# A decoder layer on one core: the row products with w_out take eight merged pairs, their weight sums formed in the gates stage and stored

## What is computed

```python
merged = (jax.nn.sigmoid(g_sb) * (o_sb @ w_branch[:SB_W])
          + jax.nn.sigmoid(g_ds) * (o_ds @ w_branch[SB_W:]))
x = x + merged @ w_out

h = rms_norm(x, ffn_norm_g)
u = causal_depthwise_conv(h @ w_up, conv_w, conv_b)
```

## Time and profile before

| | us |
|---|---|
| median of 3 runs | 1435.23 (1435.18 to 1435.26) |
| profiled execution, its own time | 1435.17 |
| its span, first to last instruction | 1433.3 |

### The profile page before, as it was taken

The page is one execution under the profiler, slowest core; times in us unless marked ns, Lnnn a source line. Parts: engine busy times, 40 slices in busy tenths (PEclk is TensorE's granted clock), DMA queues, the critical chain, the costliest instruction groups (busy, mean ns, idle before and its releaser), DMA issues.

```text
span 1433.3 us, 23700 instructions
## 1 busy us (share of the span) xinstructions
PE 1427.8 (100%) x7626; PEld 1222.9 (85%) x7626; DVE 1138.3 (79%) x1503; ACT 841.5 (59%) x1181; POOL 448.0 (31%) x493
## 2 busy tenths in 40 slices
PE   9999999999999999999999999999999999999999
PEld 7888888888888888888888888888888888888887
DVE  6778998886656566899967778777778778999998
ACT  7545667666767666666664455455554545465553
POOL 2310000333132213650025455655556555200000
PEclk9999999999999999999999999999999999999999
DMA  8565665655554545567555565566665565566664
GB/s 260 187 197 172 209 195 186 193 176 176 161 162 160 167 170 178 189 221 234 192 178 184 183 202 181 186 191 190 190 191 185 180 198 185 192 232 206 204 207 148
DMA packets 121063, 272.25 MB, mean 190 GB/s; under 512 B 10688, under 2 KB 10976, under 8 KB 121008
## 3 DMA queue, kind: packets, MB, share of 16 engines
q1 hardware_dynamic: 119936, 268.99, 58.1%
q0 software_dynamic: 896, 2.42, 0.6%
q10 hardware_dynamic: 176, 0.14, 0.0%
HBM read 269.42 MB, written 2.10 MB: 189 GB/s over the span
## 4 chain that ended last, share of the span: by engine, by line
PE 99%; DMA 0%; DVE 0%; DVEq 0%; issue 0%
PE bank L2098 98%; PE bank L2152 1%; DMA y<-in_x 0%; PE bank L2371 0%; PE bank L2412 0%; DVE y L1770 0%; PE bank L2235 0%; PE bank L2171 0%; PE bank L2213 0%; DVE y L1815 0%; DVEq L201 0%; PE bank L2220 0%; PE bank L2210 0%; PE bank L2202 0%; DVEq L529 0%
## 5 line engine op out<-in xcount | busy, mean ns | idle before, releaser
L1100 DVE TENSOR_TENSOR lo<-raw,hi 128x1024 fp32r<-128x1024 f32 (+1 forms) x342 | 444.3, 1304 | 167.0 <-ACT hi L639 166.3
L639 ACT ACTIVATE hi<-raw 128x1024 fp32r<-128x1024 f32 (+1 forms) x342 | 359.2, 1053 | 271.6 <-PE bank L2098 266.9
L2098 PE MATMUL bank<-h2T,hi 128*128 128x512 f32 x1408 | 483.3, 394 | 0.0
L2098 PE MATMUL bank<-h2T,lo 128*128 128x256 f32 x1408 | 376.8, 278 | 0.0
L2098 PEld LDWEIGHTS bank<-h2T,hi 128*128 128x128 f32 x1408 | 257.9, 188 | 53.5
L2098 PE MATMUL bank<-hT,hi 128*128 128x512 f32 (+1 forms) x784 | 272.9, 395 | 0.0
L2098 PEld LDWEIGHTS bank<-h2T,lo 128*128 128x128 f32 x1408 | 264.4, 188 | 7.8
L2098 PE MATMUL bank<-hT,lo 128*128 128x256 f32 (+1 forms) x784 | 212.6, 281 | 0.0
L2062 POOL TENSOR_TENSOR u<-u,rms_row 128x256 f32<-128x256 f32 x88 | 120.9, 1374 | 184.7 <-DVE u L1621 165.7
L2098 PE MATMUL bank<-hi,ffT 128*128 128x512 f32 x576 | 177.4, 389 | 0.0
L2098 PEld LDWEIGHTS bank<-hT,hi 128*128 128x128 f32 (+1 forms) x784 | 143.9, 187 | 29.4
(11 more groups left out here) (292 smaller groups left out, 2017.6 us busy)
## 6 DMA issues: line engine op xcount, KB each, us to landing
raw<-in_w_up SPq DMA_DIRECT2D x176, 512.0 KB, 3.5
raw<-in_w_in SPq DMA_DIRECT2D x160, 512.0 KB, 3.4
raw<-in_w_down SPq DMA_DIRECT2D x88, 512.0 KB, 4.4
raw<-in_w_branch SPq DMA_DIRECT2D x32, 512.0 KB, 3.6
raw<-in_w_out SPq DMA_DIRECT2D x24, 512.0 KB, 4.6
raw4h<-in_w_in SPq DMA_DIRECT2D x8, 512.0 KB, 3.4
raw5h<-in_w_in SPq DMA_DIRECT2D x8, 512.0 KB, 4.4
raw45m<-in_w_out SPq DMA_DIRECT2D x8, 512.0 KB, 4.9
```

Of the source, the lines that this page charges most:

```text
L639: act.activation(hi[s][:, 0:width], raw[s][:, 0:width], ACT.Copy)\
L1100: dve.tensor_tensor(lo[s][:, 0:width], raw[s][:, 0:width], hi[s][:, 0:width].bitcast(f32), ALU.subtract)\
L2098: return pe.matmul(o, l, r, start=start, stop=stop, skip_group_check=True)
```

## The change

- `OUT_SUMMED` goes from 3 to 4: four merged and four plain pairs in each block. The stage has 48 chunks for 44, and 48 raw loads for 32.
- The sums of w_out's blocks are no longer made in the out stage. In the gates stage SP loads, once a head, the four blocks of one merged pair and half into a buffer `out_pre` (1 MB in three loads, ahead of the first weight load of the group), DVE adds at j = 5 (1024 wide), 6 and 7 (512 wide each), and SP writes the 1 MB to an array in HBM, `out_sums` (ahead of the group's seventh load). Eight such turns, for four pairs and two halves. SP waits for a turn's store before the next turn's loads, and for the last before branch group 1.
- In the out stage a merged pair takes four loads: 256 KB, 512 KB, and two of 512 KB from `out_sums`. Its chunks are then all made alike.
- The order of the pairs changes, with two places in each block where two merged pairs, 0 and 1 or 2 and 3 (in block 1 only 2 and 3), follow each other. `out_sums(m, n)` is called `out_far(m, n)`; its offsets for block 0, those of `out_near` and of `square` change. For block 1 the offsets (7, 8, 9, 10) stay, counted from a pair that starts at chunk 40 of 48 for 34 of 44.
- The last eight raw loads (for the last four) rotate over slots 0 to 3.

```diff
--- before.py
+++ after.py
-    OUT_SUMMED = 3
+    OUT_SUMMED = 4
...
-    OUT_ORDER = [[("plain", 4)] + turns(0, 5, 1, 6, 2, 3) + [("plain", 7)],
-                 turns(0, 4, 1, 5, 2, 6) + [("plain", 3), ("plain", 7)]]
-    ROW_STEPS = block_steps({b: ROW_ORDER for b in S_BLOCKS}, ROWS_AT[2], 0)
+    OUT_ORDER = [[("plain", 4), ("summed", 0), ("summed", 1), ("plain", 5), ("summed", 2), ("summed", 3),
+                  ("plain", 6), ("plain", 7)],
+                 [("summed", 0), ("plain", 4), ("summed", 1), ("plain", 5), ("summed", 2),
+                  ("summed", 3), ("plain", 6), ("plain", 7)]]
...
-    ROW_SLOT += [q if q < SLOTS else q % SLOTS if q >= OUT_RAWS - SLOTS else q % (SLOTS + 2)
-                 for q in range(OUT_RAWS)]
+    ROW_SLOT += [q if q < SLOTS else q % (SLOTS + 2) if q < SLOTS + (SLOTS + 2) * OUT_EXTRA
+                 else q % SLOTS for q in range(OUT_RAWS)]
...
+        out_pre = at("out_pre", [4 * GRP], 48 * KB)
+        out_sums = nc.dram_tensor("out_sums", (2 * OUT_SUMMED * P, 4 * GRP), f32,
+                                  kind="Internal").ap()
...
-                for k in range(2):
+                for k in range(4 if step.stored else 2):
...
+                    width = GRP if step.stored and k == 0 else BLOCK
+                    if k < 2:
+                        kt = 2 * step.pair + k
+                        src = w[kt * P:(kt + 1) * P, ds(col, width)]
+                    else:
+                        row = (2 * step.pair + step.m - NB) * P
+                        src = out_sums[row:row + P, (k - 2) * BLOCK:(k - 1) * BLOCK]
+                    load(slot, raw_s[stage(step)][slot][:, 0:width], src)
...
+            def out_turn(pair, m):
+
+                i = 2 * pair + m
+                row, col = 2 * P * pair, m * BLOCK
+
+                def before(j):
+                    if j == 0:
+                        wait_alone(sp, out_stored, 16 * i + 1)
+                        sp.dma_start(out_pre[:, 0:2 * GRP], w_out[ds(row, P), col:col + BLOCK])\
+                            .then_inc(out_landed, 16)
+                        sp.dma_start(out_pre[:, 2 * GRP:3 * GRP],
+                                     w_out[ds(row + P, P), col + GRP:col + BLOCK])\
+                            .then_inc(out_landed, 16)
+                        sp.dma_start(out_pre[:, 3 * GRP:4 * GRP],
+                                     w_out[ds(row + P, P), col:col + GRP])\
+                            .then_inc(out_landed, 16)
+                    if j == 6:
+                        wait_alone(sp, out_summed, 3 * i + 3)
+                        sp.dma_start(out_sums[ds(P * i, P), :], out_pre[:, :])\
+                            .then_inc(out_stored, 16)
+                return before
+
+            prime(sp, out_stored)
+            load_group(C_GATES, w_in, 0, GATE_AT)
+            with sp.Fori(0, OUT_SUMMED - 1) as q:
+                for m in range(2):
+                    load_group(C_GATES, w_in, CPG * (2 * q + m + 1), GATE_AT + GRP * (2 * q + m + 1),
+                               before=out_turn(q, m))
+            load_group(C_GATES, w_in, CPG * 7, GATE_AT + GRP * 7, before=out_turn(OUT_SUMMED - 1, 0))
+            load_group(C_BRANCH, w_branch, 0, 0, before=out_turn(OUT_SUMMED - 1, 1))
+            wait_alone(sp, out_stored, 16 * 2 * OUT_SUMMED + 1)
+            with sp.Fori(1, 4) as g:
                 load_group(C_BRANCH, w_branch, CPG * g, GRP * g)
...
-                if 18 <= c - OUT_AT[1] < 22:
-                    square(c - OUT_AT[1] - 18)
+                if 21 <= c - OUT_AT[1] < 25:
+                    square(c - OUT_AT[1] - 21)
...
-                    first_at = step.chunk - (1 if stage(step) else 2)
-                    second_at = step.chunk + (1 if stage(step) and step.made == 1
-                                              else 0 if stage(step) else -1)
-                    b1, b2 = [raw_s[stage(step)][ROW_SLOT[step.raw + k]] for k in range(2)]
-                    s13, s24 = ssum13[stage(step)], ssum24[stage(step)]
-                    if c == first_at:
+                    b1, b2 = [raw_s[0][ROW_SLOT[step.raw + k]] for k in range(2)]
+                    s13, s24 = hsum13, hsum24
+                    if c == step.chunk - 2:
...
+                    if j == 5:
+                        dve.wait_ge(out_landed, 48 * h + 48)
+                        dve.tensor_tensor(out_pre[:, 0:2 * GRP], out_pre[:, 0:2 * GRP],
+                                          out_pre[:, GRP:3 * GRP], ALU.add).then_inc(out_summed, 1)
+                    if j == 6:
+                        dve.wait_ge(out_summed, 3 * h + 1)
+                        dve.tensor_tensor(out_pre[:, 2 * GRP:3 * GRP], out_pre[:, 0:GRP],
+                                          out_pre[:, 2 * GRP:3 * GRP], ALU.add)\
+                            .then_inc(out_summed, 1)
+                    if j == 7:
+                        dve.wait_ge(out_summed, 3 * h + 2)
+                        dve.tensor_tensor(out_pre[:, 3 * GRP:4 * GRP], out_pre[:, 2 * GRP:3 * GRP],
+                                          out_pre[:, 3 * GRP:4 * GRP], ALU.add)\
+                            .then_inc(out_summed, 1)
...
-                    weight_sums(c)
...
-                weight_sums(c)
-                for m, joins_at in enumerate(((7, 10, 16, 22), (7, 8, 9, 10))):
+                for m, joins_at in enumerate(((7, 12, 13, 18), (7, 8, 9, 10))):
                     if c - FAR_LAST[NB + m] in joins_at:
-                        out_sums(m, joins_at.index(c - FAR_LAST[NB + m]))
-                if c - OUT_AT[1] in (16, 17):
-                    for o in ((0, 1), (2, 3))[c - OUT_AT[1] - 16]:
+                        out_far(m, joins_at.index(c - FAR_LAST[NB + m]))
+                if c - OUT_AT[1] in (11, 20):
+                    for o in (0, 1) if c - OUT_AT[1] == 11 else (2, 3):
                         out_near(o)
```

More of the change, by code:

```diff
@@ L69, in hybrid_layer @@
     C_ROWS = KT // TAIL_CK
-    Step = namedtuple("Step", "m pair made chunk raw")
+    Step = namedtuple("Step", "m pair made chunk raw stored", defaults=(False,))
     S_BLOCKS = range(2, NB)
@@ L86, in hybrid_layer, with block_steps @@
     BLOCK_END = {**{b: ROWS_AT[b + 1] for b in S_BLOCKS}, NB: OUT_AT[1], NB + 1: OUT_AT[2]}
-    def block_steps(orders, chunk, raw):
+    def block_steps(orders, chunk, raw, stored):
         table = []
@@ L93, in block_steps @@
                 made = pair if kind == "summed" else None
-                table.append(Step(b, pair, made, chunk, raw + 2 * len(table)))
+                table.append(Step(b, pair, made, chunk, raw, stored and made is not None))
                 chunk += 2 if made is None else 4
+                raw += 4 if table[-1].stored else 2
             assert chunk == BLOCK_END[b]
@@ L537, in load, with load_group @@
                 sp.dma_start(dst, src).then_inc(w_landed[slot], 16)
-            def load_group(c0, w, step, col, n=CPG, width=GRP, per=CK):
+            def load_group(c0, w, step, col, n=CPG, width=GRP, per=CK, before=None):
                 for j in range(n):
+                    if before is not None:
+                        before(j)
                     wait_alone(sp, lo_done, c0 + j - AHEAD + step)
@@ L577, in load_step @@
                         wait_alone(sp, sig_done, 8 * 4)
-                    kt = 2 * step.pair + k
-                    load(slot, raw_s[stage(step)][slot][:, :],
-                         w[kt * P:(kt + 1) * P, ds(col, BLOCK)])
+                    width = GRP if step.stored and k == 0 else BLOCK
[6 more added lines that the diff above has]
+                    load(slot, raw_s[stage(step)][slot][:, 0:width], src)
             for step in ROW_STEPS:
@@ L1233, in weight_sums @@
                             dve.wait_ge(lo_done, ROW_S[n - 1].chunk + 3)
-                        dve.wait_ge(left_done, 2 * stage(step) + 2)
+                        dve.wait_ge(left_done, 2)
                         slot = ROW_SLOT[step.raw]
-                        if slot < SLOTS or stage(step):
-                            both = (raw_two + [raw45m])[slot // 2]
+                        if slot < SLOTS:
+                            both = raw_two[slot // 2]
                             dve.tensor_tensor(s13[:, :].rearrange("p (n c) -> p n c", n=2),
```

47 lines of the change are left out of this document (24 added, 23 removed).

## The result

The changed kernel takes **1439.5 us** (median of 9 runs, 1438.6 to 1440.7) against 1435.2 for the kernel before; the ratio is 1.0026, with a 95% interval of 1.0018 to 1.0035. That is slower by about 4 us (4.2 by the medians, 3.7 by the ratio), and the whole interval lies above 1. The profiled execution took 1439.72 us by its own time, the one of before 1435.17.

The account below looks back on a forecast made before the run. PE was taken to bound the kernel, busy 1427.8 of 1433.3 us. From 1435.2 us, the terms -1.4 + 0.4 + 0.7 + 0.6 + 0.8 + 2.0 = +3.1 gave 1438.3 us, range 1436.3 to 1441.0.

Parts of the forecast that it names:

- Removed matmuls: Out stage: two more merged pairs save a product of three matmuls each on PE, -1.4 us.
- The gates stage: Gates stage: the added loads, additions and stores fit in idle time and cost PE 0.
- Start of the out stage: Chunks 7 to 9 fall behind as subtractions slow while POOL mixes, +0.4 us (0 to +1).
- Load 43: End of out stage: load 43 waits for lo 39 and lands 3.5 us later; PE waits, +0.7 us (0.5 to 1.5).
- rival C: Loads bound the merged runs: 5 us a load, pairs 2 and 3 of block 0 also lose; 1440.8 us, chance 0.19.
- Far copies: End of out stage: ACT's last far copy holds up PE's eight transposes, +0.6 us (0 to 1).
- h2T: Start of up stage: PE's first chunk waits for DVE's first h2T tile, +0.8 us (0.3 to 1.3).
- banks: Up stage: PE's first transposes wait for DVE to add the near banks, +2.0 us (1 to 3).
- A: Backlog at the end of the out stage as the terms have it: 1438.3 us, 1437.0 to 1440.0, chance 0.6.
- B: End of out stage hidden, far additions fit, hi 47 3 us earlier than t = 15.4: 1434.7 us, chance 0.12.
- D: Gates stage pays 0.3 to 0.5 us a head for late bank sums or stores: 1441.3 us, chance 0.05.
- E: Nothing moves but the matmuls, no new waits at the out stage's end: 1433.8 us, chance 0.04.

Follow-up runs that it names:

- stored3: Kernel before plus the stored sums only: three merged pairs, old pair order, additions and squares at old places; 1435.9 us, ratio 0.9997.
- gates_only: Kernel before plus the change's gates-stage loads, additions and stores, with the stored sums read by nobody; 1435.5 us, ratio 1.0000.
- slots6: Changed kernel with the last eight out-stage loads kept rotating over six raw slots; 1439.5 us, ratio 1.0018.
- order2: Changed kernel with block 1's pairs reordered so the last merged pair ends two chunks earlier; 1440.4 us, ratio 1.0031.
- both: Changed kernel with six raw slots to the end and the last merged pair two chunks earlier; 1438.0 us, ratio 1.0013.
- far_last: Changed kernel with DVE's end order changed: h2T, two far-addition sets, four banks, lo 50, last two sets; 1442.7 us, ratio 1.0048.
- far_slots_order: `far_slots` with block 1's pairs ordered summed 0, plain 4, summed 1, 2, plain 5, summed 3, plain 6, 7; 1441.2 us, ratio 1.0037.
- far_slots: `far_last` with six raw slots to the end of the out stage; 1440.5 us, ratio 1.0038.
- banks_slots: Changed kernel with six slots, first h2T tiles ahead of the third far-addition set and banks ahead of the fourth; 1439.0 us, ratio 1.0021.
- spread: Changed kernel with six slots and block 1's end work (far additions, h2T tiles, squares) spread over the up stage; 1436.8 us, ratio 1.0013.

## Why the prediction came out

1438.3 us was predicted, between 1436.3 and 1441.0; 1439.5 was measured. Step by step:

- **Removed matmuls, -1.4**: right. `stored3` without waits takes 109.3 with 366 matmuls; 360 take 1.36 less.
- **The gates stage, 0**: right, by `gates_only`. SP's wait for the store was the part without a row. The store of 1 MB lands 4.7 us after its issue, as soon as the loads (4.8). The Trainium skill ("DMA: Bandwidth & Descriptors", section "Anatomy of one DMA - SWDGE (gpsimd) path") warns of a long confirmation where the target is HBM; no run here shows one beyond a load's.
- **Start of the out stage, +0.4**: wrong in sign, by 0.7 to 0.8. PE lost nothing at chunks 7 to 9, and the small waits of before (0.4) went too. I let POOL mix until 637 us as before; it ends at 633.4 now, and from 632.7 on four subtractions take 1.2 us each (the first, still beside POOL, is only 512 wide; such a one takes 0.68 elsewhere, as at 688.75; the other three are 1024 wide):

```profile
626.25 1.77 DVE L1262 TENSOR_TENSOR lo<-raw,hi 128x1024 fp32r<-128x1024 f32 x1 [0.52 <-ACT hi L767]
632.70 4.78 DVE L1262 TENSOR_TENSOR lo<-raw,hi 128x512 fp32r<-128x512 f32 x4
...
631.83 1.54 POOL L2087 TENSOR_TENSOR br<-br,br 128x256 f32<-128x256 f32 x1
```

  The Trainium skill ("SBUF - State Buffer", section "Who interferes with whom") has a VectorE instruction with two inputs in SBUF contend with a GpSimd instruction that reads SBUF. The trace agrees: 1.77 us beside POOL and 1.2 without. With DVE's sums gone POOL's mixing ends sooner too, which the step left out; `gates_only` and `stored3`, whose out stages start at the same 626.4 us, show it by the last instruction of the mixing:

```profile
637.20 1.54 POOL L2083 TENSOR_TENSOR br<-br,br 128x256 f32<-128x256 f32 x1
...
632.96 0.74 POOL L2085 TENSOR_TENSOR br<-br,br 128x256 f32<-128x256 f32 x1
```
- **Load 43, +0.7**: the step that failed in size. It measured 2.3, as 0.95 at chunk 41 and 1.36 at 43. The place and the cause (look-ahead of four slots) were right, as `slots6` shows; the landing time was not. I took 3.5 us, the median of the up stage's loads, for loads that are issued four in a row, though the 24 loads of w_out into slots 0 to 3 have a median of 4.6 us on the page of before. They took 5.0, 5.1 and 5.3 (rival C's number), and load 41 was late as well.
- **Far copies, +0.6; h2T, +0.8; banks, +2.0**: 0.3, 1.3 and 1.6, together 3.1 where 3.4 was said. DVE without a gap and the two waits that DVE ends are as predicted; the last far copy ended at 703.72 and the eight transposes started at 703.77, as predicted too, but so small a wait has no releaser in the views. `order2` and `both` show them as one thing: with the last merged pair two chunks earlier all three are gone.
- **Chunk 20, 0.3**: not in the sum. It is a late load of block 0, and one of the signs that I had named for C was there: loads issued from 636 to 648 us took 5.9 to 8.3 us. The six slots ahead covered all of it but 0.3 us here, and all but 0 to 1.4 us in the other profiles with the same block 0.

So the sum +3.1 became +4.0 in the stretch by +1.6 at the loads, -0.7 at the start, -0.3 in the backlog and +0.3 at chunk 20. The profiled time is 4.55 us above that of before; 0.4 of the rest are the last store's landing, 0.1 I can't place. The forecast held by partly cancelling errors: the true case lies between A (backlog) and C (loads), whose extra wait in block 0 came as 0.3 us and not as 1. That the total fell inside the range owes something to luck: two terms were off by 1.6 and 0.7 us in opposite directions, and a block 0 like that of `order2` would have added 1.1 us and put it near the range's upper end. B was off: hi 47 was done at 703.2, 16.8 us after the end of chunk 35, and not at 12.4, behind the late loads 41 and 43; D and E are out.

## What to carry to other kernels

When matmuls go from the end of a stage, count what the other engines must do from the last merged step to the next stage's first products, and follow every queue behind each piece: work that is only put in another order comes out as the wait of the next one in line. Price a load by rows with as many loads in flight as there will be. Test the parts of a change apart: here the stored sums alone lost nothing, and the fourth pair, with the new order and the moved additions, saved 1.4 us of matmuls and brought 5.8 us of waits.

## What was not expected of the hardware

- A gap of 2.3 us on PE (`order2`) and two of 2.9 (`far_last`, `far_slots_order`) were followed by 3.4 us at a granted clock of 0.50 (1.2 GHz), which began when PE was already working again (at 695.4 us in `order2`, where the gap ended at 694.84). Gaps of 1.4 us (changed kernel) and of 2.9 us (`far_slots`) were not, the clock stayed at 1.00. Such a wait cost 1.6 to 1.8 times its idle time where the clock fell, and whether it fell was not the same in three runs with a gap of 2.9 us.
- A load of 512 KB takes 3.4 to 3.8 us when it is alone in flight. With several in flight, issued 1.1 to 2 us apart, it mostly takes 4 to 9 us, with the DMA share at 0.86 to 1.0. The same load is not always as fast: the one of chunk 44 took 7.5, 8.8 and 6.8 us in `slots6`, `banks_slots` and `spread`, whose loads are the same. The timed runs of kernels with these loads spread over 2 to 7 us, where the kernel before stays within 2.2, save for one run. That the loads make the spread fits this, but no pair of profiles of one kernel shows it.
